# A peer-expert kernel: VectorE's order of work at the change from expert input to output products

## The reference

```python
q = (x @ w_q).reshape(T, HEADS, 2, 128)
v1, i1 = top_k(q[:, :, 0] @ k1.T, 16);  v2, i2 = top_k(q[:, :, 1] @ k2.T, 16)
top_s, pos = top_k(v1[..., :, None] + v2[..., None, :], 16)     # over the 256 pairs
idx = take_along_axis(i1 * 128 + i2, pos);  g = softmax(top_s)
h = einsum('thkd,td->thk', u_tab[idx], x)                        # u_tab: 16384 x 1024
y = einsum('thk,thkd->td', gelu(h) * g, v_tab[idx])              # v_tab: 16384 x 1024
```

## Time and profile before

| | |
|---|---|
| median of 3 runs | 2056.74 us (2055.52 to 2058.3) |
| span of the profiled execution, first to last instruction | 2055.4 us |
| what the median has over that span (the profiled execution's time outside its span isn't recorded apart) | 1.3 us |
| PE busy | 2028.8 us, 99% of the span |
| DVE, ACT, POOL busy | 61%, 50%, 69% |
| mean granted TensorE clock | 0.997 of full |
| changes from u to v | at 701.5 and at 1666.5 us |

### The profile page before, as it was taken

The page is one execution under the profiler, slowest core; times in us unless marked ns, Lnnn a source line. Parts: engine busy times, 40 slices in busy tenths (PEclk is TensorE's granted clock), DMA queues, the critical chain, the costliest instruction groups (busy, mean ns, idle before and its releaser), DMA issues.

```text
span 2055.4 us, 39515 instructions
## 1 busy us (share of the span) xinstructions
PE 2028.8 (99%) x14308; PEld 1811.5 (88%) x14308; DVE 1251.5 (61%) x2142; ACT 1030.6 (50%) x1358; POOL 1416.0 (69%) x592
## 2 busy tenths in 40 slices
PE   8999999999999999999999999999999999999998
PEld 8999999999888888888889899999988878888886
DVE  5246369912766799953337537990367689994333
ACT  5557554454555444445446665545455544444443
POOL 6656878888777777754447456888877777775442
PEclk9999999999999999999999999999999999999999
DMA  7433545555444455465555234555555444555553
GB/s 263 152 128 124 175 155 182 181 180 183 165 172 173 154 173 172 171 225 184 185 189 178 103 121 149 185 182 183 177 174 170 173 162 169 172 171 184 184 184 132
DMA packets 97299, 351.46 MB, mean 171 GB/s; under 512 B 12112, under 2 KB 12368, under 8 KB 96848
## 3 DMA queue, kind: packets, MB, share of 16 engines
q1 hardware_dynamic: 96224, 345.40, 49.2%
q10 hardware_dynamic: 1008, 5.13, 0.7%
HBM read 349.44 MB, written 1.05 MB: 171 GB/s over the span
## 4 chain that ended last, share of the span: by engine, by line
PE 95%; DVE 3%; ACT 1%; DMA 1%; issue 0%; POOL 0%; SPq 0%; ACTq 0%; POOLq 0%; DVEq 0%
PE ps L626 24%; PE ps L628 23%; PE ps L627 23%; PE ps L1027 11%; PE ps L1028 6%; PE ps L1019 3%; PE ps L915 1%; PE ps L1003 1%; DVE slo L2032 0%; DVE act L1857 0%; DMA ring<-in_weights 0%; PE ps L594 0%; DVE act L1865 0%; PE ps L815 0%; PE ps L795 0%
## 5 line engine op out<-in xcount | busy, mean ns | idle before, releaser
L560 POOL TENSOR_TENSOR wlo<-ring,whi 128x1024 fp32r<-128x1024 f32 x584 | 1408.2, 2416 | 606.9 <-ACT whi L1396 469.0
L1396 ACT ACTIVATE whi<-ring 128x1024 fp32r<-128x1024 f32 x536 | 566.4, 1060 | 780.8 <-PE ps L628 590.7
L626 PE MATMUL ps<-whi,shi 128*128 128x512 f32 x1024 | 409.5, 400 | 4.4 <-DVE act L2012 4.4
L627 PE MATMUL ps<-wlo,shi 128*128 128x512 f32 x1024 | 406.6, 397 | 0.0
L628 PE MATMUL ps<-whi,slo 128*128 128x512 f32 x1024 | 406.6, 397 | 0.0
L626 PE MATMUL ps<-hboth,whi 128*128 128x256 f32 x1392 | 395.7, 284 | 0.0
L627 PE MATMUL ps<-hboth,whi 128*128 128x256 f32 x1392 | 393.8, 283 | 0.0
L628 PE MATMUL ps<-hboth,wlo 128*128 128x256 f32 x1392 | 393.8, 283 | 0.0
L1027 PE MATMUL ps<-hboth,whi 128*128 128x512 f32 x1024 | 362.7, 399 | 0.0
L1028 PE MATMUL ps<-hboth,wlo 128*128 128x256 f32 x1024 | 285.7, 279 | 0.0
L626 PEld LDWEIGHTS ps<-hboth,whi 128*128 128x128 f32 x1392 | 267.0, 192 | 2.2 <-issue 2.0
(11 more groups left out here) (306 smaller groups left out, 2780.8 us busy)
## 6 DMA issues: line engine op xcount, KB each, us to landing
ring<-in_weights SPq DMA_DIRECT2D x651, 512.0 KB, 3.2
act<-in_const ACTq DMA_DIRECT2D x1, 2372.0 KB, 9.2
act<-in_const SPq DMA_DIRECT2D x1, 2240.0 KB, 12.6
xres<-in_x SPq DMA_DIRECT2D x4, 256.0 KB, 4.6
act<-in_keys ACTq DMA_DIRECT2D x1, 1024.0 KB, 4.7
out<-act ACTq DMA_DIRECT2D x2, 512.0 KB, 2.6
ring<-in_weights SPq DMA_DIRECT2D x2, 256.0 KB, 4.5
act<-in_fgain ACTq DMA_DIRECT2D x1, 512.0 KB, 3.3
```

What stands on the lines that cost most here:

```text
L560: pool.tensor_tensor(wlo[:, j, :], ring[:, j, :], whi[:, j, :].bitcast(F32), ALU.subtract)\
L626: pe.matmul(dst, wide[0], narrow[0], start=start, stop=False, skip_group_check=True)
L627: pe.matmul(dst, wide[0], narrow[1], start=False, stop=False, skip_group_check=True)
L1396: eng.activation(whi[:, j, :], ring[:, j, :], ACT.Copy).then_inc(hi_ready[j], 1)
```

## The change

In VectorE's stream `rest_of(1, 1)`, the remainder of pair 1, moves behind the one-hots of the second group and behind `add_low` of the last pair. Nothing is added or removed, and no other engine's stream changes.

```diff
                 rest_of(0, 0)
-                rest_of(1, 1)
                 hot(0, 1, GROUPS, 1, 1)
                 add_low(last_k, 1)
+                rest_of(1, 1)
                 eng.wait_ge(n["gelu_done"], E_TILES // 2)
                 with eng.Fori(0, HALF_ROUND - 1) as k:
```

## The result

The changed kernel takes 2045.23 us (median of 5 runs, 2044.15 to 2046.68), the kernel before 2055.52 beside it (5 runs, 2052.22 to 2058.3): ratio 0.995, 95% interval 0.9939 to 0.9961. That is 10.3 us or 0.5% faster. The forecast was 2048.7 with a range from 2046.7 to 2052.4. The kernel before is itself 1.2 us faster beside the changed one than in the three runs that the forecast started from (2056.74). So of the 3.5 us between forecast and measured time 1.2 are the starting point, and 2.3 are a gain larger than the 8.0 forecast.

The account below looks back on a forecast made before the run. TensorE, busy 99% of the span, was taken as the bound. Winning back waits and low clock, 3.94 us in the first block and 4.07 in the second, gave 2056.74 − 8.0 = 2048.7 us, range 2046.7 to 2052.4.

Parts of the forecast that it names:

- The wait: TensorE's wait for the last pair's addition at both changes from u to v, 2.28 and 2.40 us, should go altogether.
- The size of a place: Gain at each change from u to v, wait plus low clock: 3.94 us in the first block, 4.07 in the second.
- The low clock: Matmuls at 1.2 GHz behind the waits at both changes from u to v, counted as 1.66 and 1.67 us won back.
- half the gain: Rival at both changes: waits go but the clock still falls for another reason; gain 4.68 us, time 2052.1; chance 0.06.
- The moved remainder: Second remainder, started at 703.71 and 1668.86, ends at least 1.4 us before TensorE needs it for slot 2; cost nought.
- the later end: End of the second remainder if GpSimd's pass comes first: 706.70, in the second block 1671.73.
- the prediction's own bound: If VectorE comes ahead of GpSimd's pass, the second remainder ends within some 0.6 us, at 704.3.
- The slower rival: Second remainder loses three GpSimd passes, ends at 712.3; TensorE waits 4.2 us at slot 2; time 2060.6; chance 0.04.
- the 2.89 us: Length of the second remainder before the change, said to agree with VectorE's two SBUF inputs contending with GpSimd's reads.
- the sum: Gains at both changes from u to v, 8.0 us, taken off the span of 2055.4 to give 2047.4.
- the two places: The changes from u to v in the first and second block, where TensorE waits for VectorE; 8.0 us in all.
- The 1.3 us between median and span: Whole kernel: the median time was taken as 1.3 us over the profiled span, 2056.74 against 2055.4.

Follow-up runs that it names:

- Experiment 3: Kernel before with only the second group's one-hots moved ahead of the second remainder, the last addition still behind it: 2052.18 us, ratio 0.9982; run again 2049.37 us, 0.9977.

## Why the prediction was wrong, point by point

- **The wait.** Right. It said that banks 0 and 1 are free 0.53 and 0.40 us before TensorE asks; the addition started at 700.57 and took 0.6 us to the next instruction, the question came at 701.70, 0.53 us behind its end. The waits went from 2.28 and 2.40 to nothing.
- **The size of a place.** Right for this pair of profiles: 3.94 and 4.07 forecast, 3.93 and 4.07 measured.
- **The low clock as a sure part of it.** Too simple. That it fell at the changes only behind waits held in every trace, but the clock also stayed up behind 4 of the 14 long waits, and at the third place behind 5 of 18. On average it is 10/14 × 1.66 = 1.2 us a place, not 1.66. The rival "half the gain" is out: without a wait the clock never fell there in any of the profiles.
- **The moved remainder.** Right that it costs nothing. I took the later end (706.70); it came first, ahead of GpSimd's pass, as in the prediction's own bound. The start that the prediction worked out, 703.71, already lay ahead of GpSimd's 703.81. The slower rival, three lost passes, never showed. GpSimd ran 0.5 us late, as said, and nothing waited.
- **What the wait was made of.** The prediction described the 2.89 us as GpSimd's pass and still treated the whole order as the cause. Experiment 3 shows that moving the one-hots alone takes the wait to 0.07 and 0.20 us. VectorE and GpSimd meet here without any semaphore between them.
- **The step that failed: the sum.** "2055.4 − 8.0 = 2047.4 us of span" took everything outside the two places as equal. It left out a term for the rounds with L1027 and L1028, whose slow cadence was in the profile of before for one block, 3.37 us. That term less the 0.8 us of a later start makes up what the span has under the forecast (2047.4 − 2044.9 = 2.5). The page that I worked from showed the mean of the two (399 and 279 ns), and I never held the two blocks beside each other. In the profiles a wait at a change goes with a slow block in 15 of 20 cases. By my estimate a place is then worth 2.34 of wait + 1.2 of clock + 0.75 × 3.37 = 2.5 of cadence, some 6 us; two are 12, and the ratios of the changed kernel, 0.9945 and 0.995, are 11.3 and 10.3 us. The estimate is 1 to 2 us high, before any part of the third place. The shares of 20 blocks are rough, and likely too high: in 6 of the 12 later profiles of kernels with a wait the profiled execution was the slowest or second slowest of its kernel's 11 or 12 runs.
- **The starting point.** The forecast stood on a median of three runs, 2056.74; beside the changed kernel the same program gave 2055.52 in five. From there the same 8.0 us would have given 2047.5, still 2.3 too high. The 1.3 us between median and span mixes two executions: in the runs where both are on record the time is 1.8 us over the span.
- **The range.** Its low end was the forecast less 2 us of scatter, and its high end, 2052.4, is 0.3 over the prediction's own half gain, 2052.1. The kernel before alone scatters over 7 us (2052.02 to 2059.06 in one batch) and the changed one over 2.8 us (2043.84 to 2046.68). That difference in scatter was the sign of terms of several us that come and go, which the three runs shown before, 2055.52 to 2058.3, could only hint at.

## What to carry to other kernels

Two remainders back to back cost 4.7 us here, because each met a pass of the engine that reads the same memory, and one outside such a pass 0.7; look for the gap between such passes before reordering for priority, and give each of several results its own due time. When one stage occurs twice in a trace, lay the two beside each other: a stage that runs at two rates is a term of its own, and it can gain or lose more than the edit. Where a term comes and goes, profile one program several times before trusting the terms of one trace. And price a wait of the bounding engine by an experiment that puts it in, since here 0.3 and 0.4 us of wait cost some 6.

## What the runs showed of the hardware that I had not expected

- The pair of a 512-column and a 256-column matmul ran at 0.346 or 0.353 us. In every profile a block's first tile ran in the slow cadence, and the choice showed right behind the first 32 gate matmuls, then held for all 15 rounds that followed.
- The slow cadence came only in blocks with a wait for the addition at the change before (15 of 20, against 0 of 16), for waits from 0.07 to 2.60 us.
- The granted clock fell to 1.2 GHz behind 10 of 14 waits of 2.28 to 2.60 us, and stayed at full behind the other 4; behind the wait of 2.23 to 2.25 us at the third place it fell in 13 of 18 profiles. By the rule of the Trainium skill ("TensorE: Matmul & The Clock Gate", "Why this matters for your kernels") gaps so short should leave it alone; the measurements differ.
- Which of VectorE and GpSimd comes first decides which of them is long: VectorE's remainder took 0.67 us and GpSimd's pass 2.85 when VectorE started 0.08 us earlier, 2.89 and 2.40 when it started 0.05 later. That agrees with what the Trainium skill ("SBUF — State Buffer", "Who interferes with whom") says of two SBUF inputs.
